# Moving five of eleven modulation rounds of a four-layer kernel: two to a later projection, three to a feed-forward

## The chip, the cores and the metric

One core of a Trainium2 chip runs the whole program. The metric is the device time of one launch in microseconds, median of the runs shown.

## What is computed

Four residual layers act on 256 tokens of width 1024; layers 0 and 1 also carry 256 context tokens, layer 2 uses the context for keys and values only. All is fp32. Each layer has a conditioning vector `c` and a modulation of six rows of 1024, three pairs of which are called rounds 0, 1 and 2 here:

```python
mods = silu(c) @ ada_w[i] + ada_b[i]          # [1024] @ [1024, 6144]
sh1, sc1, g1, sh2, sc2, g2 = split(mods, 6)
h = norm(x) * (1 + sc1) + sh1
x = x + g1 * mixer(h)                         # rounds 0 and half of 1
x = x + g2 * ffn(norm(x) * (1 + sc2) + sh2)   # rest of 1, and 2
```

Mixers and feed-forwards, in order: layer 0, two linear recurrences with one input projection (3616 wide) and a mixture of 32 experts; layer 1, differential attention (projection 3072 wide) and 32 experts; layer 2, latent attention with a Fourier mix, and a dense SwiGLU of width 2816; layer 3, convolutions, and a dense SwiGLU. Rounds (0,1), (0,2), (1,0) and (2,0) are needed for two conditioning vectors (`c` and the context's), all others for one.

## The kernel before, in words

The stages run one after the other; a stage ends for all engines together. Weights come through a ring of six slots of 1 MiB (`self.ring`). The order of everything in the ring is a list that is written at build time (`self.W`, by `plan_...`); SyncE works through it in `feed` (L285 to L295), and before each load it waits until the slot's earlier content is used up. `frees` and `self.released` give slots back in the order in which TensorE's program comes to them.

A round of modulation is eight units of 1 MiB (128 rows of `ada_w`, 2048 columns). Two stages host rounds beside their own projection, both through `st_linear_hosting` (L426): the first projection (called AB here, 28 groups of eight 128x512 matmuls, four groups to a chunk of two ring slots), and the second (called C, 20 groups, the first two chunks of two groups). `hosted` (L384) spreads the units over the groups by a cost of 3, or 5 for a unit of two vectors that VectorE sums. Behind a group, TensorE's program comes to the units given to it:

- a round in `on_pe` is multiplied on TensorE (L471, four matmuls a unit, 32 columns of the array each), and its slot comes free by that;
- any other round is summed on VectorE: `weigh` (L569) takes one instruction of 128x2048 per unit and vector (L575 for the first, L577 for the seven others); the slot comes free when it is done. When all eight are summed, `add_up` (L479) on TensorE adds over the partitions with four matmuls a vector (L486).

Then `take` (L581) adds the bias on VectorE, and GpSimd's queue stores the two rows to a scratch in HBM (L548), after which it may load the next bias (L544). `load_mod` (L608) reads rows back, spread over all partitions, when a later stage needs them: in AB and C by SyncE behind the feed (L525, L526), in the latent attention (L2367) for layer 3. In C, VectorE also normalizes four tiles at the start (L566, L567), and turns angles for rotary embedding at groups 4, 5, 12 and 13 (L808 to L814), in program order with the units.

The AB stage hosts seven rounds (rounds number 0 and 5 of the list on TensorE), C four (number 0 on TensorE). The mixture of experts begins with its own stage (`moe`, L1282): SyncE's loads (L1356, L1360), GpSimd's parameters, and VectorE, whose first act is `mod_here`, a wait for every `load_mod` issued so far.

The feed-forward `ffn` (L2652) has 11 blocks j. TensorE does `gateup(j+1)` (64 records, L2677) and then `down(j)` (16 records, L2689); ScalarE's silu (L2740) and VectorE's product (L2754) lie between. VectorE begins the stage with `entry_begin` (L2564), which needs rows 0 and 1 of layer 3.

A matmul of fp32 stands as two records in the trace, so a group of eight is 16 records.

## Time and profile before

| | |
|---|---|
| median of 3 runs | 2607.36 us (2604.98 to 2614.38) |
| span of the profiled execution | 2609.1 us; no time of its own is recorded for it |
| TensorE busy | 2251.0 us, 86% |
| VectorE busy | 814.0 us, 31% |
| DMA, mean | 268 GB/s |
| AB stage | 59.7 to 292.7 us |
| C stage | 1032.5 to 1195.6 us |
| start stage of the second mixture | 1283.0 to about 1331 us |
| first feed-forward, blocks | 2027 to 2248 us |

The page gives busy times and the span in slices; a stage has its own limits, so the rows below are taken stage by stage. Idle time is that of the named engine ahead of an instruction, with what ended it. `PEclk` is the granted TensorE clock as a share of 2.4 GHz.

### The profile page before, as it was taken

How to read it: one execution, taken by the hardware profiler on the slowest of the kernel's cores; microseconds unless marked ns; L12 is line 12 of the kernel's file. 1: busy time of each engine (PE TensorE's matmuls, PEld its weight loads, DVE VectorE, ACT ScalarE, POOL GpSimd, SP SyncE). 2: the span in 40 equal slices, each digit the busy share in tenths (PEclk: the TensorE clock that was granted, in tenths of full speed). 3: DMA queues.
4: the chain of work that ended last, by engine and by line, in shares of the span. 5: the costliest groups of instructions: out<-in, count | busy, mean ns of one | idle time of the engine just before them, and what ended most of it. 6: DMA issues, size and time to landing. Idle time of an engine off the chain costs nothing. (4 is left out here: it accounts for less than half of the span.)

```text
span 2609.1 us, 35238 instructions
## 1 busy us (share of the span) xinstructions
PE 2251.0 (86%) x14123; PEld 1215.0 (47%) x14124; DVE 814.0 (31%) x1504; ACT 371.3 (14%) x623; POOL 125.7 (5%) x182
## 2 busy tenths in 40 slices
PE   6999969798888882897778788887699999989999
PEld 3333564443343331344442223322455777766776
DVE  2483575520000006375652200000443000393001
ACT  0000222111111111003321111111042000010000
POOL 0000011000000002100100000000210000000000
PEclk8999989899999995999989999999799999999999
DMA  8889712699999984884179999998441544534442
GB/s 286 315 327 349 284 33 67 267 419 423 423 423 422 423 362 171 295 333 187 52 295 423 423 422 423 423 422 370 158 154 41 186 145 161 166 118 130 161 145 81
DMA packets 176765, 698.24 MB, mean 268 GB/s; under 512 B 14085, under 2 KB 72325, under 8 KB 114096
## 3 DMA queue, kind: packets, MB, share of 16 engines
q1 hardware_dynamic: 162512, 648.98, 64.1%
q0 software_dynamic: 8512, 25.83, 3.0%
q10 hardware_dynamic: 5664, 22.37, 2.4%
q8 instruction: 53, 0.87, 0.1%
q14 instruction: 24, 0.20, 0.0%
HBM read 673.87 MB, written 22.20 MB: 267 GB/s over the span
## 5 line engine op out<-in xcount | busy, mean ns | idle before, releaser
L1571 PE MATMUL bank<-ring,arena 128*32 128x512 f32 (+1 forms) x3072 | 357.0, 613 | 76.9 <-DMA ring<-moe_w_up 50.0
L503 PE MATMUL bank<-ring,actT 128*128 128x512 f32 x768 | 344.4, 607 | 11.8 <-issue 7.6
L2677 PE MATMUL bank<-actT,ring 128*128 128x256 f32 x1344 | 293.3, 379 | 0.0
L2677 PEld LDWEIGHTS bank<-actT,ring 128*128 128x128 f32 x1344 | 255.2, 190 | 42.3 <-issue 8.6
L1571 PEld LDWEIGHTS bank<-ring,arena 128*32 128x32 f32 x3072 | 100.5, 112 | 328.4 <-issue 327.1
L1588 PE MATMUL bank<-arena 128*32 128x512 f32 (+1 forms) x2048 | 226.6, 594 | 25.7 <-ACT arena L1662 24.7
L503 PEld LDWEIGHTS bank<-ring,actT 128*128 128x128 f32 x768 | 147.1, 194 | 209.4 <-issue 205.2
L1703 DVE TENSOR_TENSOR arena<-arena,bank 128x512 f32<-128x512 f32 x32 | 22.0, 687 | 612.3 <-ACT arena L1660 612.3
L577 DVE SCALAR_TENSOR_TENSOR arena<-ring,cols,arena 128x2048 f32<-128x2048 f32 x70 | 163.3, 2350 | 58.0 <-DMA ring<-ada_w 56.4
L2039 PEld LDWEIGHTS bank<-arena 128*128 128x128 bf16 x2448 | 141.4, 100 | 32.3 <-issue 26.8
L2689 PE MATMUL bank<-ring,arena 128*128 128x512 f32 x352 | 154.3, 592 | 0.0
L2039 PE MATMUL bank<-arena 128*128 128x128 bf16 x2448 | 147.3, 223 | 4.8 <-DVE arena L1695 4.8
L1588 PEld LDWEIGHTS bank<-arena 128*32 128x32 f32 x2048 | 65.7, 110 | 165.1 <-issue 165.1
L1571 PE MATMUL bank<-actT,arena 128*32 128x512 f32 (+1 forms) x1024 | 116.3, 594 | 30.1 <-DMA actT<-moe_w_up 30.1
L2754 DVE TENSOR_TENSOR arena<-arena,bank 128x512 f32<-128x512 f32 x22 | 15.1, 687 | 402.0 <-ACT arena L2740 402.0
L2689 PEld LDWEIGHTS bank<-ring,arena 128*128 128x128 f32 x352 | 66.9, 190 | 75.7 <-issue 74.6
L1317 PE MATMUL bank<-ring,actT 128*128 128x512 f32 x192 | 83.6, 594 | 4.0 <-DMA arena<-moe_b_rexp 1.8
L1660 ACT ACTIVATE arena<-bank 128x512 f32<-128x512 f32 x32 | 19.1, 597 | 468.4 <-PE bank L1571 468.4
L1571 PEld LDWEIGHTS bank<-actT,arena 128*32 128x32 f32 x1024 | 32.0, 110 | 112.7 <-issue 112.7
L556 ACT ACTIVATE arena<-bank 128x512 f32<-128x512 f32 x48 | 28.7, 597 | 369.1 <-PE bank L503 369.1
L2740 ACT ACTIVATE arena<-bank 128x512 f32<-128x512 f32 x22 | 13.1, 597 | 408.6 <-PE bank L2677 408.6
L1709 DVE TENSOR_TENSOR arena<-bank,mod 128x512 f32<-128x512 f32 x32 | 20.6, 686 | 158.6 <-PE bank L1588 158.6
(446 smaller groups left out, 2045.0 us busy)
## 6 DMA issues: line engine op xcount, KB each, us to landing
ring<-moe_w_gate SPq DMA_DIRECT2D x128, 1024.0 KB, 24.1
arena<-moe_w_down SPq DMA_DIRECT2D x128, 1024.0 KB, 21.8
ring<-ada_w SPq DMA_DIRECT2D x96, 1024.0 KB, 8.0
ring<-ffn_w SPq DMA_DIRECT2D x66, 1024.0 KB, 5.3
ring<-moe_w_up SPq DMA_DIRECT2D x64, 1024.0 KB, 23.8
actT<-moe_w_up SPq DMA_DIRECT2D x64, 1024.0 KB, 24.6
made_scratch<-arena ACTq DMA_DIRECT2D x32, 512.0 KB, 7.7
ring<-ab_w_in SPq DMA_DIRECT2D x14, 1024.0 KB, 7.2
```

The source lines that it names most:

```text
L503: mm = nc.tensor.matmul(self.bank[g % 6][:, :], lhsT(m, k), halves[k // 4][:, k % 4, :], start=(k == 0), stop=(k == KT - 1))
L556: nc.scalar.activation(dest(*groups[g]), self.bank[g % 6][:, :], ACT.Copy).then_inc(self.act_done.up(), 1)
L577: ins = nc.vector.scalar_tensor_tensor(total(n, v), w, c, total(n, v), ALU.mult, ALU.add)
L1317: mm = nc.tensor.matmul(proj_bank(t, c)[:, :], tok(t, 4 * j + k), halves[c][j][:, k, :], start=(j == 0 and k == 0), stop=(j == 1 and k == 3))
L1571: mm = nc.tensor.matmul(bank[j // 2][Q * q:Q * q + Q, :], A(XS + P * kt + Q * q, Q), weights(j, own, q, k * DE, DE), start=(kt == 0), stop ...
L1588: mm = nc.tensor.matmul(bank[4 + half][Q * q:Q * q + Q, :], A(HT + P * (2 * j + f) + Q * q, Q), weights(4 + j, own, q, f * D + half * 512, ...
L1660: nc.scalar.activation(A(SG, 512), bank[0][:, :], ACT.Silu).then_inc(sc["silu"], 1)
L1703: V_.tensor_tensor(A(HH, 512).rearrange("p (j f q) -> p j f q", f=2, q=P), self.by_rows(A(SG, 512)), self.by_rows(bank[1][:, :]), ALU.mult ...
L1709: ins = V_.tensor_tensor(A(YS + half * 512, 512), bank[4 + half][:, :], self.mod_row(5)[:, half * 512:half * 512 + 512], ALU.mult)
L2039: mm = self.nc.tensor.matmul(self.bank[2 + k // 4][:, P * (k % 4):P * (k % 4) + P], part(i)[:, t * D + k * P:t * D + (k + 1) * P], pick[:, ...
L2677: mm = nc.tensor.matmul(bank[2 - 2 * (j % 2) + which][:, f * SEQ:(f + 1) * SEQ], w[:, k, f * P:(f + 1) * P], self.actT[:, k * T:k * T + SE ...
L2689: return nc.tensor.matmul(acc(t, half)[:, :], A(H + 512 * (j % 2) + f * SEQ + t * P, P), w[:, f, half * 512:(half + 1) * 512], start=(j == ...
```

## The change

AB hosts five rounds instead of seven, one of them on TensorE. C hosts the three rounds of layer 2, all on VectorE, the first of them for two vectors. The three rounds of layer 3 are summed on VectorE inside the first feed-forward, from four buffers of their own that GpSimd's queue fills. Layer 3's rows 0 and 1 are now loaded by ScalarE's queue in that feed-forward, and `entry_begin` comes behind its blocks; layer 2's rows 0 and 1 are loaded at the start of the second mixture instead of at the end of C.

```diff
-AB_ROUNDS = [(0, 1), (0, 2), (1, 0), (1, 1), (1, 2), (2, 0), (2, 1)]
+AB_ROUNDS = [(0, 1), (0, 2), (1, 0), (1, 1), (1, 2)]
-C_ROUNDS = [(2, 2), (3, 0), (3, 1), (3, 2)]
+C_ROUNDS = [(2, 0), (2, 1), (2, 2)]
+FFN_ROUNDS = [(3, 0), (3, 1), (3, 2)]
-AB_ON_PE, C_ON_PE = (0, 5), (0,)
+AB_ON_PE, C_ON_PE = (0,), ()
+AB_HOMES, C_HOMES = ((0, 1), (2, 3), (0, 1), (2,), (0,)), ((0, 1), (2,), (0,))
...
     # st_linear_hosting
-        total = lambda n, v: self.A(sums + 2048 * ((on_dve.index(n) % 2) * max(vecs) + v), 2048)
+        total = lambda n, v: self.A(sums + 2048 * homes[n][v], 2048)
...
                     self.load_mod(sp, 1, 2, 6, (0,))
-                    self.load_mod(sp, 2, 0, 2, (0,))
...
     # moe, SyncE
                 if layer == 0:
                     self.load_mod(sp, 1, 0, 2, (0, 1))
+                else:
+                    self.load_mod(sp, 2, 0, 2, (0,))
...
     # mixer_mla, SyncE
-                self.load_mod(sp, 3, 0, 2, (0,))
...
     # ffn, TensorE; CLOSED = (3, 6, 9)
+                def add_up(r, to):
+                    pe.wait_ge(ada_summed.sem, ada_summed.at(KT * (r + 1)))
+                    for b in range(4):
+                        mm = nc.tensor.matmul(to[32 * b:32 * b + 32, :], self.ones[:, 0:32], total[:, 512 * b:512 * b + 512], start=True, stop=True)
+                    mm.then_inc(ada_done.up(), 1)
...
                     if j + 1 < n:
                         gateup(j + 1)
+                    if rounds and j in CLOSED:
+                        pe.wait_ge(h_ready.sem, h_ready.at(j + 1))
+                        add_up(CLOSED.index(j), bank[2 - 2 * (j % 2)])
                     down(j)
+                    if rounds and j in CLOSED:
+                        pe.wait_ge(ada_added.sem, ada_added.at(CLOSED.index(j) + 1))
...
     # ffn, GpSimd
+                def ask(i):
+                    r, k = units[i]
+                    layer, third = rounds[r]
+                    if i >= 4:
+                        pool.wait_ge(ada_summed.sem, ada_summed.at(i - 3))
+                    w = self.I["ada_w_2"][layer % 2]
+                    pool.dma_start(unit(i), w[k * P:(k + 1) * P, 2048 * third:2048 * (third + 1)]).then_inc(self.unit_in[i % 4], 16)
...
+                for r in range(len(rounds)):
+                    for k in range(KT):
+                        ask(KT * r + k)
+                        if k == 4:
+                            bias(r)        # waits for the store of round r-1
+                        if r and k == 2:
+                            store(r - 1)   # waits for take(r-1)
...
     # ffn, ScalarE
+                    if rounds and j == 6:
+                        act.wait_ge(ada_stored.sem, ada_stored.at(32))
+                        self.load_mod(act, rounds[0][0], 0, 2, (0,))
...
     # ffn, VectorE
-                if then_row is not None:
-                    self.entry_begin(dve, link, 0)
                 for j in range(n):
...
+                    if rounds:
+                        if j in CLOSED:
+                            take(CLOSED.index(j), bank[2 - 2 * (j % 2)][:, :])
+                        for i in range(len(units)):
+                            if (0, 0, 1, 1, 1, 2, 2, 2)[i % KT] + 3 * (i // KT) == j:
+                                weigh(i)
+                if then_row is not None:
+                    self.entry_begin(dve, link, 0)
```

## Rows read from the trace of the kernel before

**Rows 1.** Busy time by stretch: PE, PEld, DVE, ACT, POOL, clock, DMA share, GB/s.
```profile
59.70:292.70 233.00, 222.02 (x632) 90.14 (x632) 127.36 (x66) 16.12 (x27) 26.58 (x50) 0.98 0.89 325
125.40:155.50 30.10, 29.34 (x80) 12.59 (x81) 29.48 (x15) 2.38 (x4) 1.16 (x2) 1.00 0.89 317
190.60:222.50 31.90, 31.79 (x72) 13.23 (x72) 23.05 (x11) 1.81 (x4) 3.17 (x6) 0.91 1.00 392
1032.50:1195.60 163.10, 155.39 (x408) 63.52 (x408) 84.26 (x58) 12.84 (x21) 17.75 (x33) 0.96 0.80 291
2048.00:2247.70 199.70, 199.70 (x753) 142.62 (x751) 11.46 (x19) 5.97 (x10) 0.00 (x0) 1.00 0.47 153
```
**Rows 2.** Groups of instructions by line, AB stage.
```profile
L503 PE MATMUL bank<-ring,actT 128*128 128x512 f32 x448 | 201.0, 607 | 10.6 <-issue 7.6 <-DMA ring<-ab_w_in 1.8 <-PEq L628 1.3
L577 DVE SCALAR_TENSOR_TENSOR arena<-ring,cols,arena 128x2048 f32<-128x2048 f32 x49 | 113.9, 2349 | 31.8 <-DMA ring<-ada_w 30.6
L471 PE MATMUL bank<-ring,scx 128*32 128x512 f32 x128 | 15.6, 599 | 1.5 <-DMA ring<-ada_w 1.5
L575 DVE TENSOR_SCALAR arena<-ring,cols 128x2048 f32<-128x2048 f32 x7 | 8.8, 1285 | 48.5 <-DMA ring<-ada_w 48.5
L486 PE MATMUL bank<-arena,misc 128*32 128x512 f32 x24 | 3.2, 600 | 0.0
```
**Rows 3.** Timeline of TensorE in AB: start, length, what, idle before.
```profile
141.91 34.60 PE L503 MATMUL bank<-ring,actT 128*128 128x512 f32 x80
190.65 16.86 PE L503 MATMUL bank<-ring,actT 128*128 128x512 f32 x32 [5.22 <-issue]
263.80 20.84 PE L503 MATMUL bank<-ring,actT 128*128 128x512 f32 x48 [1.80 <-DMA ring<-ab_w_in]
```
**Rows 4.** What SyncE's queue waited for, 60 to 320 us.
```profile
SPq L294 <- DVE arena L577: 97.0, 27, 7.4
```
**Rows 5.** DMA issues of the same stretch; the second row of 60 to 105 us.
```profile
ring<-ada_w SPq DMA_DIRECT2D x52, 1024.0 KB, 7.6
...
mod<-k_ret POOLq DMA_DIRECT2D x1, 2048.0 KB, 13.5
```
**Rows 6.** Groups of instructions by line, C stage.
```profile
L471 PE MATMUL bank<-ring,scx 128*32 128x512 f32 x64 | 9.8, 716 | 7.7 <-DMA ring<-ada_w 7.7
```
**Rows 7.** Timeline of TensorE in C, around its long wait.
```profile
1065.57 1.93 PE L471 MATMUL bank<-ring,scx 128*32 128x512 f32 x8 [7.17 <-DMA ring<-ada_w]
...
1069.90 9.01 PE L503 MATMUL bank<-ring,actT 128*128 128x512 f32 x16
...
1080.69 7.13 PE L503 MATMUL bank<-ring,actT 128*128 128x512 f32 x16
```
**Rows 8.** Timeline of VectorE, C stage.
```profile
1079.65 1.23 DVE L808 TENSOR_TENSOR arena<-arena 128x1024 f32<-128x1024 f32 x1 [37.17 <-ACT arena L556]
```
**Rows 9.** Timeline of VectorE, start of the first mixture, then of the second.
```profile
406.20 2.50 DVE L1421 TENSOR_SCALAR xres<-xres 128x1024 f32<-128x1024 f32 x4 [12.38 <-DMA mod<-mods_scratch]
412.64 1.22 DVE L1424 SCALAR_TENSOR_TENSOR arena<-mod,arena 128x1024 f32<-128x1024 f32 x1 [3.94 <-DMA arena<-moe_b_rexp]
...
1283.00 1.29 DVE L1421 TENSOR_SCALAR xres<-xres 128x1024 f32<-128x1024 f32 x2 [0.37 <-PEq L628]
1295.56 1.23 DVE L1424 SCALAR_TENSOR_TENSOR arena<-mod,arena 128x1024 f32<-128x1024 f32 x1 [11.26 <-DMA arena<-moe_b_rexp]
...
1310.74 0.69 DVE L1439 TENSOR_TENSOR arena<-bank,mod 128x512 f32<-128x512 f32 x1 [0.25 <-PE bank L1317]
```
**Rows 10.** Timeline of SyncE's queue, start of the first mixture.
```profile
396.75 1.15 SPq L612 DMA_DIRECT2D mod<-mods_scratch  x2
```
**Rows 11.** Timeline of TensorE, first feed-forward.
```profile
2075.47 13.98 PE L2677 MATMUL bank<-actT,ring 128*128 128x256 f32 x64
2089.28 7.03 PE L2689 MATMUL bank<-ring,arena 128*128 128x512 f32 x16
```
**Rows 12.** Who waited for whom, 2010 to 2262 us.
```profile
DVE arena L2754 <- ACT arena L2740: 195.6, 11, 20.0
```

More of the change, by code:

```diff
@@ L238, in __init__ @@
         self.cleared = ctx.enter_context(nc.semaphore("cleared"))
+        self.unit_in = [ctx.enter_context(nc.semaphore(f"unit_in{n}")) for n in range(4)]
     def signals(self, *names):
@@ L424, in plan_ada, with st_linear_hosting @@
         self.plan(w[k * P:(k + 1) * P, 2048 * r:2048 * (r + 1)].rearrange("(k p) n -> p k n", p=P), 1, 2048)
-    def st_linear_hosting(self, lhsT, chunks, dest, rounds, sums, on_pe=(), lead=0, unmix=None, tables=None, beside=None):
+    def st_linear_hosting(self, lhsT, chunks, dest, rounds, sums, homes, pick, on_pe=(), lead=0, unmix=None, tables=None, beside=None):
         nc, sm = self.nc, self.sem
@@ L483, in add_up @@
                     for v in range(vecs[n]):
-                        ones = self.ones[:, 0:32] if vecs[n] == 1 else self.A(PICK + 16 * (1 - v), 32)
+                        ones = self.ones[:, 0:32] if vecs[n] == 1 else self.A(pick + 16 * (1 - v), 32)
                         for j in range(4):
@@ L568, in _ @@
                     ins.then_inc(sm["x_normed"].up(), 1)
+                    dve.wait_ge(sm["x_normed"].sem, sm["x_normed"].at(1))
                 def weigh(n, l, r, k):
@@ L586, in _ @@
                 if 2 in vecs:
-                    nc.vector.memset(self.A(PICK, 16), 0.0)
-                    nc.vector.memset(self.A(PICK + 32, 16), 0.0)
-                    nc.vector.memset(self.A(PICK + 16, 16), 1.0)
+                    nc.vector.memset(self.A(pick, 16), 0.0)
+                    nc.vector.memset(self.A(pick + 32, 16), 0.0)
+                    nc.vector.memset(self.A(pick + 16, 16), 1.0)
                 for g in range(len(groups)):
@@ L2252, in raise_sums @@
             nc.scalar.activation(A(LAM, 16), A(LAM, 16), ACT.Exp).then_inc(lam_exp.up(), 1)
-        self.st_linear_hosting(lambda m, k: self.actT[:, k * T + m * P:k * T + m * P + P], C_CHUNKS, dest, C_ROUNDS, C_SUMS, C_ON_PE, lead=2, unmix=A(XX, 2048),
+        self.st_linear_hosting(lambda m, k: self.actT[:, k * T + m * P:k * T + m * P + P], C_CHUNKS, dest, C_ROUNDS, C_SUMS, C_HOMES, C_PICK, C_ON_PE, lead=2, unmix=A(XX, 2048),
                                beside=dict(pool=load_tables, dve=turn_angles, act=raise_sums))
@@ L2650, in plan_ffn, with ffn @@
                 self.plan(I["ffn_w2_2"][l][(j - 1) * H:j * H, :].rearrange("(k p) n -> p k n", p=P), 2, D)
-    def ffn(self, l, then_row):
+    def ffn(self, l, then_row, rounds=()):
         nc, I, A, bank, sm = self.nc, self.I, self.A, self.bank, self.sem
         SG, H = 2048, 3072
+        ada_done, ada_added, ada_bias, ada_stored, ada_summed = (sm[k] for k in ("ada_done", "ada_added", "ada_bias", "ada_stored", "ada_summed"))
+        units = [(r, k) for r in range(len(rounds)) for k in range(KT)]
+        unit = lambda i: A(FFN_UNITS + 2048 * (i % 4), 2048)
+        total = A(FFN_SUM, 2048)
+        kept = self.scx[:, 512:1024]
+        CLOSED = (3, 6, 9)
         acc = lambda t, c: bank[4 + 2 * t + c]
@@ L2747, in _, with weigh, take @@
                 link = self.linker(dve, self.dve_chain)
-                if then_row is not None:
-                    self.entry_begin(dve, link, 0)
+                def weigh(i):
+                    r, k = units[i]
+                    layer = rounds[r][0]
+                    dve.wait_ge(self.unit_in[i % 4], 16 * (i // 4 + 1))
+                    c = self.cols[:, 16 * (layer // 2) + k:16 * (layer // 2) + k + 1]
+                    if k == 0:
+                        ins = nc.vector.tensor_scalar(total, unit(i), c, None, ALU.mult)
+                    else:
+                        ins = nc.vector.scalar_tensor_tensor(total, unit(i), c, total, ALU.mult, ALU.add)
+                    ins.then_inc(ada_summed.up(), 1)
+                    dve.wait_ge(ada_summed.sem, ada_summed.total)
+                def take(r, of):
+                    dve.wait_ge(ada_bias.sem, ada_bias.at(64 * (r + 1)))
+                    dve.wait_ge(ada_done.sem, ada_done.at(r + 1))
+                    nc.vector.tensor_tensor(kept, of, kept, ALU.add).then_inc(ada_added.up(), 1)
                 for j in range(n):
@@ L2755, in _ @@
                                             ALU.mult).then_inc(h_ready.up(), 1)
+                    if rounds:
+                        if j in CLOSED:
[3 more added lines that the diff above has]
+                                weigh(i)
+                if then_row is not None:
+                    self.entry_begin(dve, link, 0)
                 if then_row is not None:
@@ L2995, in run @@
         self.mixer_mla()
-        self.ffn(0, I["norm1_g_2"][1])
+        self.ffn(0, I["norm1_g_2"][1], FFN_ROUNDS)
         self.mixer_conv()
```

22 lines of the change are left out of this document (20 added, 2 removed).

## The prediction

> **What bounds the kernel now.** The page first: TensorE is busy 86% of the span, VectorE 31%, and the DMA mean is far under what the two expert stages reach. That says little, because the change touches only stretches, so I read the busy times by stretch next [rows 1]. In the AB stage TensorE works 222.0 of 233.0 us, in C 155.4 of 163.1 us, in the blocks of the first feed-forward all of 199.7 us. So in all three the end is set by TensorE's own program plus its waits; nothing that only VectorE or the DMA queues do is paid for, unless it makes TensorE wait.
>
> Then the same two hosting stages by line. In AB a group of eight matmuls costs 34.60 / 5 = 6.9 us at full clock [rows 3], 28 of them 194 us; a unit on TensorE is 15.6 / 16 = 0.98 us, an `add_up` of one vector 3.2 / 3 = 1.07 us; VectorE takes 2.35 us per unit and vector, 1.29 us for the first of a round [rows 2]. The rest is waits and slow clock. In the timeline the long wait, 5.22 us, lies ahead of a chunk's first group, and the two groups behind it take 16.86 instead of 13.9 us [rows 3]; the granted clock of that stretch is 0.91 (of 2.4 GHz), after TensorE had stood still [rows 1]. Why the chunk was late: loads are in order, and SyncE stood 97 us for slots that VectorE held [rows 4]; between 125 and 155 us VectorE was busy 29.5 of 30.1 us, and between 190 and 222 us the DMA moved 392 GB/s at a share of 1.00 [rows 1]. First VectorE, then the DMA engines limit the stream; TensorE feels it at the chunks.
>
> **AB stage.** Two rounds go, 16 MiB of 70.
> - Round (2,0) leaves TensorE: 8 x 0.98 = 7.8 us.
> - Round (2,1) leaves VectorE, and its `add_up` TensorE: 1.1 us.
> - Waits, 233.0 - 222.0 = 11.0 us, and 2.9 us of slow clock behind the long one. By the costs in `hosted`, all units together now weigh 152 instead of 200 over the same 26 groups. In the two-vector part that is 1.17 units a group instead of 1.54, 5.5 us of VectorE per 6.9 us instead of 7.2: VectorE keeps up. In the one-vector part it is 8 units and 2 slots of weights per chunk of four groups, 10.5 MB in 27.5 us = 380 GB/s, just under the 392 measured; so I don't expect all waits to vanish. I keep 4 us of the 11 and take 7 + 2.9 = 9.9 us off. Bounds: 0 (nothing of the wait goes) and 13.9.
> Sum AB: 7.8 + 1.1 + 9.9 = 18.8 us. Behind AB everything starts earlier by this; the stage barrier and the stores of the last round follow as before.
>
> **C stage.** Round (2,2) leaves TensorE: the row gives 9.8 us busy and 7.7 us of waits for its eight units [rows 6]; the 7.17 us wait is one of these, and the group behind it took 9.01 instead of 7.13 us [rows 7], 1.9 us. With no unit on TensorE all three go: 19.4 us. Added: four vectors to add up instead of three, 1.07 us. VectorE now sums 32 instead of 24 vector-units, 18.8 us more, but it had stood still 37.2 us at the start of this stage [rows 8] and was busy 84 of 163 us [rows 1].
> What is late next is a chain: a slot of round (2,0) is filled (7.6 us to landing [rows 5]), summed for two vectors (4.7 us), and only then filled again, 12.3 us a turn. Counting the release order, units 1, 3, 5 and 7 form such a chain from the end of the first chunk (1048 us): four turns, 49 us, plus two turns of angles of 3.7 us, 1105 us; TensorE asks for the sum (`add_up` behind group 9) at about 1103 us. A second such chain ends about 2 us ahead of the last `add_up`. Bounds for the stall: 0, and 10 us if each turn meets a queue like the 13.5 us of the big table [rows 5]; I take 3, from the median landing. Sum C: 19.4 - 1.1 - 3 = 15.3 us.
> The Trainium skill, "SBUF — State Buffer", section "The DMA setup-cost knee", has 2 us plus the bytes over 436 GB/s for such a transfer, 4.4 us for a unit; by that estimate a turn is 9.1 us, the stall is zero, and the total would be 3 us better. The trace's 7.6 us is a median with other loads in flight, and I go by it.
>
> **Feed-forward.** TensorE's blocks have no gap: 13.98 and 7.03 us follow each other [rows 11]. Three `add_up`s go in between: 3 x 1.07 = 3.2 us, all on the path. The rest lies beside: VectorE waited 195.6 us of the stage [rows 12]; per block of 20.7 us it now gets at most three units, 7.1 us. In blocks 3, 6 and 9 it also stands in `take` until `gateup(j+1)` and `add_up` are through, but the next product is needed only after `down(j)` and another `gateup`, over 20 us later, and `take` itself (0.7 us) ends inside `down(j)` (7 us), before TensorE waits for it. DMA: 3 MiB per block more, 153 + 152 GB/s of the 392 seen; a ring load has two blocks of lead. `entry_begin` moves behind the blocks, where VectorE waits for `down(10)`; its rows are loaded from block 6 on, four blocks early. The removed load in the latent attention was in nobody's way: 0. Bounds: 3.2 and, if each `add_up` also costs a handshake as long as `take` and its silu-to-product step, 6.
> Here a page speaks against the change. First the row: the first product of a unit takes 1285 ns, the other kind 2349 ns for the same 2048 columns [rows 2]. The Trainium skill, "SBUF — State Buffer", section "SBUF: two separate sides", says that DMAs issued by GpSimd can't get their descriptors written while VectorE runs in its faster two-port modes. By that rule three instructions of 1.29 us could hold back unit loads, 3.9 us if all of it reached TensorE, total 2584 us; by the slack above it is zero, and I take zero.
>
> **Second mixture.** The load of rows 0 and 1 of layer 2 used to lie at the end of C; now it is issued when the stage starts, ahead of the two expert loads, and VectorE's first act waits for it. The first mixture shows just this: two half loads, together as large, issued at 396.75 us [rows 10]; VectorE went on at 406.20 us, and the parameters behind were in at 412.64 us, 15.9 us after the start [rows 9]. In the second they were in 12.6 us after the start (1283.0 to 1295.56 us) [rows 9]. So parameters come 3.3 us later, and VectorE's chain of normalizing, transposing and routing has 0.25 us of slack against TensorE's projection [rows 9]. Cost 3 us; bounds 0 and 4.
> The added wait for VectorE's own instruction in C (`x_normed`) is one semaphore, 0.1 us at most: nothing.
>
> **Sum.** 18.8 + 15.3 - 3.2 - 3 = 27.9 us, 1.07%. The profiled span is 2609.1 us, 1.7 over the median of the runs shown; I take the gain off both: span 2581 us, median 2607.4 - 27.9 = 2579.5 us.
>
> **Rivals.**
> - *The summing chain bounds C.* For: (2,0) with two vectors comes first there, ropes lie between its units, and the chain above had no slack. Against: VectorE has idle time. Priced with 10 us of stall at the first and 4 at the second sum, C gives 4.3 us, total gain 16.9: 2590 us.
> - *AB's waits stay.* For: 380 GB/s needed is near 392 reached, and late chunks bring slow clock with them. Against: a fifth fewer units in every stretch. AB gives 8.9 us only, gain 18.0: 2589 us.
> - *All cover holds.* No wait left in AB, no stall in C, the mixture's parameters not delayed: 22.8 + 18.3 - 3.2 = 37.9 us, 2569.5 us.
> - *The units come too slowly in the feed-forward (slower than before).* GpSimd's queue feeds 24 MiB there; a unit is due every 6.9 us (20.7 / 3). The one large load of that queue took 13.5 us for 2 MiB [rows 5], 6.8 us per MiB if one followed the other, hardly under the limit. If they serialize and take 10 us each, a block is 30 instead of 20.7 us, eight blocks lose 74 us: 2654 us. It decides from about 6.9 us per unit in series; slower than before it is from 8.4 us on. Against: four units may be in flight, so one may take 25 us from ask to sum, and the DMA share in the stage is 0.47 [rows 1]. The descriptor rule above would be a cause for it, but 3.9 us in all don't reach it.
>
> **How the numbers follow.** Forecast 0.68, chain in C 0.13, waits in AB 0.09, all cover 0.06, slow units 0.04. The measurement tells about 0.5% (13 us) from no change. Forecast and full cover are faster (0.74); the two that halve the gain are faster by 17 to 18 us in their middle, and I count 0.13 of their 0.22 as over 13 us: faster 0.87, same 0.09, slower 0.04. The range 2566 to 2596 holds all the forecast's bounds that don't fall together and the two halved cases.
>
> **What would show it.** AB about 214 us long, without the low clock near its fourth chunk; no TensorE instruction at the on-array unit line in C, and C about 148 us; the wait ahead of `add_up` in C under 5 us; in the feed-forward three short matmul groups and no idle TensorE, blocks else at 20.7 us; in the second mixture a wait of 9 to 12 us for the modulation load and routing some 3 us later after its stage's start. It is wrong if TensorE waits for sums or products in the feed-forward, if C is over 155 us, or if AB keeps its 11 us of waits.

## The result, and the profile after

The changed kernel takes 2572.2 us (median of 4 runs, 2568.0 to 2578.8), the kernel before beside it 2607.5 us (4 runs, 2605.0 to 2614.4). The ratio is 0.9865, 95% interval 0.985 to 0.988: 35.3 us less, clear of noise though under 2%. The forecast was 2579.5 us, 27.9 us faster, in a range of 2566 to 2596.

| | before | after |
|---|---|---|
| span of the profiled execution | 2609.1 us | 2566.2 us (its time 2568.0 us) |
| TensorE busy | 2251.0 us | 2226.7 us |
| VectorE busy | 814.0 us | 865.3 us |
| DMA, mean | 268 GB/s | 272 GB/s |

Busy time by stretch after: AB, C, the blocks of the first feed-forward. The columns are those of [rows 1].
```profile
58.70:269.30 210.60, 210.58 (x560) 88.11 (x560) 108.47 (x55) 16.14 (x27) 20.21 (x38) 0.99 0.76 277
1008.50:1156.40 147.90, 143.95 (x352) 61.41 (x352) 100.37 (x68) 12.85 (x21) 15.77 (x27) 0.99 0.73 262
2001.70:2205.30 203.60, 203.60 (x777) 142.92 (x776) 63.45 (x45) 5.97 (x10) 18.00 (x33) 1.00 0.74 262
```
In AB the 11.0 us in which TensorE stood still are gone to the last tenth, and its clock is 0.99. In C it stands still 4 us in all. In the feed-forward it still never does, though the DMA share went from 0.47 to 0.74.

TensorE in AB around what was the long wait, after; it answers to [rows 3].
```profile
154.74 48.33 PE L508 MATMUL bank<-ring,actT 128*128 128x512 f32 x112
203.00 1.92 PE L491 MATMUL bank<-arena 128*32 128x512 f32 x16
204.86 27.73 PE L508 MATMUL bank<-ring,actT 128*128 128x512 f32 x64
```
Seven groups in 48.33 us are 6.9 us each, and no row carries a bracket with idle time.

TensorE in C, after; it answers to [rows 7].
```profile
1008.48 27.70 PE L508 MATMUL bank<-ring,actT 128*128 128x512 f32 x64 [1.15 <-PEq L1905]
1037.31 41.44 PE L508 MATMUL bank<-ring,actT 128*128 128x512 f32 x96 [1.12 <-DMA ring<-c_w_qkv]
...
1081.56 3.22 PE L491 MATMUL bank<-arena 128*32 128x512 f32 x16 [2.82 <-DVE arena L583]
1084.70 34.96 PE L508 MATMUL bank<-ring,actT 128*128 128x512 f32 x80
```
The wait of 7.17 us for `ada_w` has gone with its instruction. New are 1.12 us for a weight, and 2.82 us for VectorE ahead of the first `add_up`.

VectorE in C, after, at the start of the sums.
```profile
1040.08 9.27 DVE L583 SCALAR_TENSOR_TENSOR arena<-ring,cols,arena 128x2048 f32<-128x2048 f32 x4 [19.07 <-DMA ring<-ada_w]
1049.71 4.62 DVE L583 SCALAR_TENSOR_TENSOR arena<-ring,cols,arena 128x2048 f32<-128x2048 f32 x2 [0.36 <-DMA ring<-ada_w]
```
It had the first unit of (2,0) early and stood 19 us for the second, then found the next ones ready: what was late was one landing.

DMA issues between 1005 and 1045 us, after: how many, KB each, median us to landing.
```profile
ring<-ada_w SPq DMA_DIRECT2D x3, 1024.0 KB, 17.1
arena<-xres POOLq DMA_DIRECT2D x4, 256.0 KB, 3.9
ring<-c_w_qkv SPq DMA_DIRECT2D x1, 1024.0 KB, 14.7
arena<-c_lq POOLq DMA_DIRECT2D x2, 256.0 KB, 8.2
arena<-c_lk POOLq DMA_DIRECT2D x2, 256.0 KB, 11.3
scx<-ada_b POOLq DMA_DIRECT2D x4, 64.0 KB, 10.2
```
A unit took 17.1 us here against the 7.6 us of [rows 5]; GpSimd's own transfers (tables, the residual, biases) were in flight beside it.

TensorE in the first feed-forward, after; it answers to [rows 11].
```profile
2049.96 13.98 PE L2690 MATMUL bank<-actT,ring 128*128 128x256 f32 x64
2063.86 1.07 PE L2723 MATMUL bank<-arena,misc 128*32 128x512 f32 x8
2064.86 7.13 PE L2702 MATMUL bank<-ring,arena 128*128 128x512 f32 x16
```
The first `add_up` lies between `gateup` and `down`; the two others look the same.

VectorE, then TensorE, at the start of the second mixture, after; they answer to [rows 9].
```profile
1249.02 1.30 DVE L1429 TENSOR_SCALAR xres<-xres 128x1024 f32<-128x1024 f32 x2 [6.13 <-DMA mod<-mods_scratch]
1257.79 1.23 DVE L1432 SCALAR_TENSOR_TENSOR arena<-mod,arena 128x1024 f32<-128x1024 f32 x1 [7.47 <-DMA arena<-moe_b_rexp]
```
```profile
1243.27 13.97 PE L1323 MATMUL bank<-ring,actT 128*128 128x512 f32 x32 [1.10 <-PEq L634]
1257.73 14.00 PE L1323 MATMUL bank<-ring,actT 128*128 128x512 f32 x32 [0.49 <-DMA arena<-moe_b_rexp]
```
The parameters are in 14.5 us after the stage's start (1243.27 us), 12.6 us before the change.

Lengths of the stretches, from TensorE's timelines: each runs from its first matmul to the first of the next stretch, so it holds the barrier behind it too and is a little longer than the windows above. M1 is the second mixture's start up to the first matmul that gathers tokens for the experts, MLA the latent attention up to the feed-forward's blocks.

| kernel | AB | C | M1 | MLA | FFN blocks | span |
|---|---|---|---|---|---|---|
| before | 234.4 | 165.7 | 48.5 | 193.3 | 223.2 | 2609.1 |
| after | 212.4 | 149.7 | 50.1 | 186.7 | 226.9 | 2566.2 |
| forecast of the difference | -18.8 | -15.3 | +3 | 0 | +3.2 | -27.9 |
| measured | -22.0 | -16.0 | +1.6 | -6.6 | +3.7 | -42.9 |

The remaining 3.6 us lie in stretches without an edit (each differs by up to 2.8 us, both ways). One of them is more than scatter: in the first mixture TensorE waits 3.3 to 3.9 us for the parameters in all seven kernels whose AB hosts five rounds with one of them on TensorE, and 1.7 to 2.1 us in the other seven (3.79 in after, 1.81 in before); in after the two groups behind it also take 15.70 instead of 14.00 us. The change costs 2 to 3 us there, which the forecast does not have; what delays the load is open. The MLA stretch was between 186.7 and 193.5 us long in the profiles of the fourteen kernels of this study, which in it differ by one load that nobody waits for, so I don't count its 6.6 us to the change. The edited stretches give 32.7 us; the medians differ by 35.3. Edited stretches vary as well: AB is 209.4 to 212.4 us long in the seven kernels that have after's AB, and C 148.0 to 149.7 in the three that have after's C (after, one_buffer, two_buffers). Much of that is the clock at a stage's start: AB's first group took 8.89 us in before and 10.16 in after, where 7.11 is the shortest, and C's first took 8.91 in before, where after's first four took 6.9 each.

### The profile page after: what moved, and what is told of

Read it like the earlier page. It is cut to its first block and busy times, and to the rows that moved or that the text cites. A ratio compares the mean times of both kernels' runs of the same rounds, so it can differ in the third digit from the quotient of the medians.

```text
span 2566.2 us, 35098 instructions
## 1 busy us (share of the span) xinstructions
PE 2226.7 (87%) x14019; PEld 1206.6 (47%) x14020; DVE 865.3 (34%) x1531; ACT 371.1 (14%) x623; POOL 140.3 (5%) x206
## 5 line engine op out<-in xcount | busy, mean ns | idle before, releaser
L508 PE MATMUL bank<-ring,actT 128*128 128x512 f32 x768 | 336.9, 599 | 4.0 <-PEq L634 1.8
L2831 DVE TENSOR_TENSOR arena<-arena,bank 128x512 f32<-128x512 f32 x22 | 15.1, 687 | 297.0 <-ACT arena L2799 297.0
L1323 PE MATMUL bank<-ring,actT 128*128 128x512 f32 x192 | 85.6, 605 | 6.5 <-DMA arena<-moe_b_rexp 4.3
L2799 ACT ACTIVATE arena<-bank 128x512 f32<-128x512 f32 x22 | 13.1, 597 | 410.9 <-PE bank L2690 410.9
```

The source lines that it names most:

```text
L508: mm = nc.tensor.matmul(self.bank[g % 6][:, :], lhsT(m, k), halves[k // 4][:, k % 4, :], start=(k == 0), stop=(k == KT - 1))
L1323: mm = nc.tensor.matmul(proj_bank(t, c)[:, :], tok(t, 4 * j + k), halves[c][j][:, k, :], start=(j == 0 and k == 0), stop=(j == 1 and k == 3))
```

## The experiments

"Before" and "after" stand for the two kernels. Kernels that were timed together share their runs of before: 2606.1 us (11 runs) for the first four; 2609.3 (17) for unit_earlier, one_buffer, two_buffers and mod_early; 2607.2 (9) for both, quiet_start, combined and combined_all. The lengths of all of them:

| kernel | AB | C | M1 | FFN blocks | span | ratio to before |
|---|---|---|---|---|---|---|
| c_hosts_six | 209.4 | 213.2 | 50.1 | 223.3 | 2630.5 | 1.012 (1.0103 to 1.0137) |
| ab_keeps_seven | 234.6 | 142.6 | 49.9 | 226.9 | 2585.2 | 0.9929 (0.9915 to 0.9942) |
| small_loads | 225.8 | 163.8 | 50.5 | 223.2 | 2623.4 | one run |
| one_vector | 234.6 | 166.2 | 50.2 | 223.2 | 2603.4 | one run |
| unit_earlier | 232.1 | 165.3 | 48.5 | 223.2 | 2607.2 | 0.9987 (0.9978 to 0.9997) |
| both | 221.6 | 166.5 | 48.5 | 223.2 | 2590.6 | one run |
| one_buffer | 210.9 | 148.7 | 50.2 | 236.1 | 2582.7 | one run |
| two_buffers | 211.0 | 148.0 | 50.2 | 226.9 | 2570.5 | one run |
| mod_early | 211.0 | 147.8 | 50.5 | 226.9 | 2572.7 | 0.9878 (0.986 to 0.9896) |
| quiet_start | 211.6 | 146.3 | 50.1 | 226.9 | 2571.1 | one run |
| combined | 209.4 | 146.1 | 50.4 | 226.9 | 2569.1 | 0.9861 (0.9843 to 0.9879) |
| combined_all | 206.3 | 146.6 | 50.6 | 226.9 | 2564.6 | 0.985 (0.9831 to 0.9869) |

### Is the feed-forward the better host? (c_hosts_six)

```diff
-C_ROUNDS = [(2, 0), (2, 1), (2, 2)]
+C_ROUNDS = [(2, 0), (2, 1), (2, 2), (3, 0), (3, 1), (3, 2)]
-self.ffn(0, I["norm1_g_2"][1], FFN_ROUNDS)
+self.ffn(0, I["norm1_g_2"][1])
```


> The changed kernel with layer 3's three rounds in the second projection (C, now six rounds, all on VectorE) and none in the feed-forward. My theory: C is then bound by its stream. 48 units and 12 weight slots are 63 MB, 157 us at the 400 GB/s seen, and VectorE has 56 x 2.35 = 132 us of sums plus some 28 us of its own; so the stage goes from 149.7 us to 165 to 175, the feed-forward gets its 3.7 us back, and the total is 12 to 21 us over the changed kernel, about 2584 to 2593. Rival: the feed-forward is only a parking place and VectorE's idle time in C would have covered the sums; then C stays within 3 us and the total is some 3 us under the changed kernel, 2569.

Measured: 2635.5 us; C is 213.2 us, 63.5 more than with three rounds. The expectation missed it by over 40 us, the stage by 38. TensorE's waits in C, from its timeline:
```profile
1065.60 3.64 PE L491 MATMUL bank<-arena 128*32 128x512 f32 x16 [10.40 <-DVE arena L583]
1091.98 8.70 PE L508 MATMUL bank<-ring,actT 128*128 128x512 f32 x16 [7.78 <-DVE scx L590]
...
1144.34 9.82 PE L508 MATMUL bank<-ring,actT 128*128 128x512 f32 x16 [8.44 <-DVE scx L590]
...
1176.18 9.27 PE L508 MATMUL bank<-ring,actT 128*128 128x512 f32 x16 [7.09 <-DVE scx L590]
```
L590 is `take`. A round now closes every three or four groups, and TensorE, which may not go on with the projection until an earlier round's bank has been taken, stands behind a VectorE that is still summing the next units; each of the three stops shown is followed by a group of 8.7 to 9.8 us instead of 7.1. VectorE has hardly any slack left itself: of the 213 us it is busy 155.5 and stands 39.0 for units to land. So the feed-forward is the better host by 59.8 us, and that is measured; why is in part argued. Over 60 us between two sums, own buffers beside the ring, and a VectorE with time to spare all come with that place, and no run takes them apart.

### The parts added one by one (ab_keeps_seven)

```diff
-AB_ROUNDS = [(0, 1), (0, 2), (1, 0), (1, 1), (1, 2)]
+AB_ROUNDS = [(0, 1), (0, 2), (1, 0), (1, 1), (1, 2), (2, 0), (2, 1)]
-C_ROUNDS = [(2, 0), (2, 1), (2, 2)]
+C_ROUNDS = [(2, 2)]
```


> The changed kernel with all seven rounds left in the first projection as before (two of them on TensorE), one round in C and three in the feed-forward: the change without the relief of AB. My theory: AB is the larger half of the gain, so AB is 234 us again instead of 212.4, C with one light round about 143 instead of 149.7, total 15 us over the changed kernel, about 2587, which is 20 us under the kernel before. Rival: the gain comes from taking work out of C and from quieter DMA later on, AB alone is worth little; then the total is within 5 us of the changed kernel.

Measured: 2587.6 us, AB 234.6, C 142.6. The two rounds that leave AB take 234.6 - 212.4 = 22.2 us with them and cost C 149.7 - 142.6 = 7.1 us; the difference, 15.1 us, agrees with that of the medians, 2587.6 - 2572.2 = 15.4 (16.7 by the ratios, each to its own runs of before). AB's long wait stands where it stood, with 5.35 us.

### What made AB wait? (small_loads, one_vector, unit_earlier, both)

My prediction said: first VectorE, which holds the slots, then the DMA engines. Three kernels take one supposed cause each out of the kernel before.

small_loads leaves out three quarters of each unit that AB hosts (so later sums have other values, tokens go to other experts, and only the AB column can be compared):
```diff
+            if i in self.ab_units:
+                dst, src = dst[:, :, 0:512], src[:, :, 0:512]
```


> The kernel before, in which the hosted units of the first projection load only 512 of their 2048 columns, all instructions kept; three quarters of seven rounds' modulations are therefore not the reference's, and so the experts' routing may differ: only the length of the AB stage (234.4 us before, first group to the next stage's first matmul) is read. If the bytes of the stream make TensorE wait, its 11 us of waits and the slow clock behind them go: 220 to 222 us. If the slots that VectorE holds for its sums make it wait, most stay: 228 us or more.

one_vector leaves the second vector's products and sums out in AB:
```diff
-                    for v in range(vecs[n]):
+                    for v in range(1 if unmix is None else vecs[n]):
```


> The kernel before, in which VectorE sums only the first vector of the two-vector rounds of the first projection (the context's modulation is left wrong, so routing may differ; only the AB stage is read); loads as before, 40 instead of 56 vector-units. If VectorE's holding of slots is what delays the weights, the waits go: 220 to 224 us. If the bytes do, the stream still asks 390 GB/s in the second half and the 5 us wait ahead of a chunk stays: 230 us or more.

unit_earlier computes all, with one unit behind group 14 instead of group 15:
```diff
+        if groups == 28 and len(rounds) == 7:
+            share[14], share[15] = share[14] + 1, share[15] - 1
```


> The kernel before, in which one hosted unit of the first projection moves from behind group 15 to behind group 14 (3 and 2 instead of 2 and 3); nothing else. Theory of slot order: slots are given back in program order, and with three units behind the last group of a chunk the second half of the next chunk's weights gets a slot of the chunk in work, which is free only when that is done; so the 5.2 us wait ahead of group 16 and the slow clock behind it (2.9 us) come from that alone, and the AB stage falls from 234.4 to 226 to 228 us, the total by 6 to 8 us to about 2599. Rival: the wait is the bytes or VectorE; then moving one unit by one group changes under 1 us.

TensorE ahead of the chunk after the long one, in before; then the long waits in small_loads, in one_vector and, with the one that follows, in unit_earlier.
```profile
223.97 7.10 PE L503 MATMUL bank<-ring,actT 128*128 128x512 f32 x16 [1.53 <-issue]
```
```profile
186.72 15.67 PE L506 MATMUL bank<-ring,actT 128*128 128x512 f32 x32 [5.23 <-issue]
```
```profile
189.88 16.05 PE L503 MATMUL bank<-ring,actT 128*128 128x512 f32 x32 [6.00 <-issue]
```
```profile
186.17 13.97 PE L505 MATMUL bank<-ring,actT 128*128 128x512 f32 x32 [0.90 <-issue]
...
220.90 9.31 PE L505 MATMUL bank<-ring,actT 128*128 128x512 f32 x16 [5.83 <-issue]
```
Half of VectorE's work on the two-vector rounds gone: the wait is 6.00 instead of 5.22 us, AB as long as before. So VectorE's hold on the slots was not the cause, and that step of the prediction is wrong. Less data: the small waits for loads are gone (one of 0.83 us for ScalarE is left), and the long one stays, 5.23 against 5.22 us; AB is 225.8 us, between the two expectations. One unit moved by one group: the long wait is 0.90 us, and the two groups behind it run at full clock (13.97 instead of 16.86 us); but now the next chunk is late, 5.83 instead of 1.53 us, and only 2.3 us of stage are left as gain where 6 to 8 were expected, 0.13% of the kernel, which the interval just tells from nothing.

Why one group matters is in the list of loads. By the costs in `hosted`, three units stand behind group 15, the last of its chunk. With the two slots of the chunk in work and the first half of the next that is all six slots, so the next chunk's second half could be asked for only when the chunk in work was through; TensorE then waits for that load, whatever VectorE or the bytes do. The trace of before shows it: SyncE's second load of weights (184 to 185.7 us), and what its queue waited for between 170 and 195 us.
```profile
185.47 0.38 SPq L294 DMA_DIRECT2D ring<-ab_w_in  x1
```
```profile
SPq L294 <- PE bank L503: 8.3, 1, 8.3
```
The last group of the chunk ended at 178.30 + 7.13 = 185.43 us, the load was issued at once and landed in 5.1 us: that is the wait of 5.22. VectorE was not behind then; at 179.61 and 182.18 us it stood itself for units. The table of [rows 4], which gave the prediction its 97 us, also has waits on these matmuls (45.9 us in 7 times), and the prediction passed over them. Behind this wait lies the second limit, the bytes. If both are all there is, taking both away leaves nothing:

> The kernel before with the two earlier edits together: the seventeenth hosted group gets one unit more and the next one less, and the hosted one-vector and two-vector units bring only 512 of their 2048 columns (the instructions stay, so sums are not those of the reference). If the waits of the first stage have two causes that cover for each other (slot order at the chunk of group 16, bytes at the chunk of group 20 and at the later ones), no wait over 0.7 us and no slow stretch stay behind the stage's start, and it is 234.4 - 11 - 3 = 220 us long (217 to 223). If one cause stands behind all, it is as with the better of the two alone, 226 us. If a third one (VectorE's pace) takes over, waits stay at group 16 or 24 and it is above 226 us.

Measured: AB 221.6 us. The only wait of TensorE inside AB in both:
```profile
250.23 20.84 PE L508 MATMUL bank<-ring,actT 128*128 128x512 f32 x48 [0.86 <-ACT arena L561]
```
The two edits by themselves save 2.3 and 8.6 us, together 12.8: the two causes cover for each other, and there is no third of any size. The stage's first group hides part of it: it took 8.89 us in before, 7.11 in small_loads, one_vector and unit_earlier, 10.17 in both. Without that group the savings are 0.5 and 6.8 us, together 14.1. The change removes both at once, since `hosted` then puts at most two units behind any group, and 16 MiB fewer come. That is why no wait at all was left.

### How much cover do the units have in the feed-forward? (one_buffer, two_buffers)

```diff
-unit = lambda i: A(FFN_UNITS + 2048 * (i % 4), 2048)
+unit = lambda i: A(FFN_UNITS + 2048 * (i % 1), 2048)     # i % 2 in two_buffers
-                    if i >= 4:
-                        pool.wait_ge(ada_summed.sem, ada_summed.at(i - 3))
+                    if i >= 1:
+                        pool.wait_ge(ada_summed.sem, ada_summed.at(i))
```


> The changed kernel with one buffer instead of four for the units in the first feed-forward. A unit then costs its landing and its sum in series, 9.9 + 2.35 = 12.3 us or, without others in flight, some 6 + 2.35 = 8.4 us, where one is due every 6.9 us. Theory: 24 units take 200 to 290 us instead of the 186 us of nine blocks, so the feed-forward (226.9 us) grows by 30 to 100 us, and TensorE waits for sums and products. Rival: VectorE's slack of 20 us per block is enough to hide even that; then it stays within 3 us.

> The changed kernel with two buffers instead of four. A unit may then take (9.9 + 2.35) / 2 = 6.1 us, just under the 6.9 us at which it is due. Theory: the feed-forward stays within 3 us of 226.9 us, so four buffers are more cover than is needed. Rival: the waits of GpSimd's queue for the stores between rounds break the flow, and it grows by 5 to 20 us.

Units of `ada_w` from GpSimd's queue between 1990 and 2260 us, with one, two and four buffers.
```profile
arena<-ada_w POOLq DMA_DIRECT2D x23, 1024.0 KB, 5.4
```
```profile
arena<-ada_w POOLq DMA_DIRECT2D x22, 1024.0 KB, 6.7
```
```profile
arena<-ada_w POOLq DMA_DIRECT2D x20, 1024.0 KB, 9.2
```
Two buffers: 226.9 us, as with four. One: 236.1 us, 9.2 more, where I had expected at least 30. With one buffer each unit costs 5.4 us of landing and 2.35 us of sum, 24 x 7.75 = 186 us, still under the 200 us of the blocks. VectorE stands 126.8 us for units and comes late to a product (L2831) that TensorE waits for ahead of two `add_up`s:
```profile
2138.26 1.94 PE L2723 MATMUL bank<-arena,misc 128*32 128x512 f32 x8 [4.30 <-DVE arena L2831]
...
2206.28 1.07 PE L2723 MATMUL bank<-arena,misc 128*32 128x512 f32 x8 [1.83 <-DVE arena L2831]
```
The waits are 6.1 us; a slower `add_up` and `down` behind the first (1.94 and 9.15 us) make up the rest. The expectation took 9.9 us, the landing with four in flight, for its high end and some 6 us for its low end, and its 30 us of growth are more than even its own 200 - 186 us give. Two buffers are not as good as four for VectorE, whose wait for units grows from 3.3 to 34.0 us; only TensorE does not feel it. VectorE's waits with two buffers and with four, between 1975 and 2225 us:
```profile
DVE arena L2818 <- DMA arena<-ada_w: 34.0, 14, 4.8
```
```profile
DVE arena L2818 <- DMA arena<-ada_w: 3.3, 4, 1.1
```
For the rival of slow units: it was to decide from 6.9 us per unit in series. With one buffer a unit costs 7.75 us in series, beyond that bound, and TensorE pays 9.2 us, not 24 x 0.85 = 20. The bound was too strict: the code asks for eight units in three blocks, 62 us, which is 7.75 us a unit.

### The load at the second mixture (mod_early)

```diff
                     self.load_mod(sp, 1, 2, 6, (0,))
+                    sp.wait_ge(ada_stored.sem, ada_stored.at(32))
+                    self.load_mod(sp, 2, 0, 2, (0,))
```
(and no load at the mixture's start)

> The changed kernel with the load of layer 2's rows 0 and 1 back at the end of the second projection (behind a wait for their store). Theory: at the start of the second mixture the load holds up the parameters and VectorE, so that start stage (50.1 us from its first matmul to the first expert's) falls to 48 us and the 0.5 us wait of TensorE there goes; total 1.5 to 3 us less. Rival: 48.5 and 50.1 are only two draws of one length; then it stays within 49 to 51 us.

Measured: 2575.3 us, M1 50.5 us, no gain. TensorE at the start of the mixture, in mod_early and in before:
```profile
1241.81 29.69 PE L1325 MATMUL bank<-ring,actT 128*128 128x512 f32 x64 [1.10 <-PEq L636]
```
```profile
1283.00 27.70 PE L1317 MATMUL bank<-ring,actT 128*128 128x512 f32 x64 [1.10 <-PEq L628]
```
The wait for parameters is gone (0.74 and 2.36 us ahead of the transposes, as before, where after has 1.21 and 2.74), and 1.6 us with it. But the projection itself takes 2.0 us longer, behind the same idle 1.10 us and with the same instructions. The granted clock is 0.86 in its first 14.2 us, where before and after have 1.00. The two later kernels with this edit show the same (29.66 and 29.86 us). But the edit need not be the cause: small_loads and one_vector, which have before's mixture, took 29.68 and 29.41 us with the clock at 0.86 and 0.88, and unit_earlier and both took 27.70. So the start stage without the load is 48.5 us long at full clock and 50.2 to 50.6 at the slow one; the delay that I priced at 3 us costs 1.6 against the first and nothing against the second, and taking it away brought nothing here.

### C's late landing, and a better version (quiet_start, combined, combined_all)

```diff
                     pool.wait_ge(sm["x_normed"].sem, sm["x_normed"].at(1))
+                    pool.wait_ge(self.pe_done.sem, self.pe_done.at(3))
```


> The changed kernel, with GpSimd's own transfers at the start of the second hosting stage held until TensorE has done its third group. If these transfers are what made the second unit of (2,0) land 17 us after its issue, it now lands within 9 us, VectorE's wait of 19 us for it falls to 10 or less, TensorE's waits of 1.12 us (c_w_qkv) and 2.82 us (sum of (2,0)) go, and the stage is 145 to 147 us instead of 149.7. If the ring's own loads crowd each other, the landing stays at 15 us or more and the stage at 148 to 150 us. Held too long, the table's late arrival would show as VectorE waiting for it at the angles of group 4.

Measured: C 146.3 us, 3.4 less than after, but 1.7 less than two_buffers, which has after's C. VectorE waits 9.14 us for the second unit, not 19.07, and later 8.57 us for another:
```profile
1032.01 9.27 DVE L584 SCALAR_TENSOR_TENSOR arena<-ring,cols,arena 128x2048 f32<-128x2048 f32 x4 [9.14 <-DMA ring<-ada_w]
1049.84 4.61 DVE L584 SCALAR_TENSOR_TENSOR arena<-ring,cols,arena 128x2048 f32<-128x2048 f32 x2 [8.57 <-DMA ring<-ada_w]
```
```profile
1010.37 68.91 PE L508 MATMUL bank<-ring,actT 128*128 128x512 f32 x160 [1.18 <-PEq L1906]
1081.69 1.92 PE L491 MATMUL bank<-arena 128*32 128x512 f32 x16 [2.42 <-DVE arena L584]
```
The second unit's landing was crowded by GpSimd's transfers: VectorE waits 18.0 to 19.7 us for it in the four kernels that have three rounds in C and keep them at the start (after, mod_early, one_buffer, two_buffers), 9.1 to 11.2 in the three that hold them. The crowding then falls on a later unit. The unit behind the 8.57 us, SyncE's queue and its landing, between 1030 and 1038 us, while GpSimd issued its held transfers from 1031.8 us on:
```profile
1036.65 0.33 SPq L299 DMA_DIRECT2D ring<-ada_w  x1
```
```profile
ring<-ada_w SPq DMA_DIRECT2D x1, 1024.0 KB, 13.1
```
The weight's wait and the slower `add_up` (3.22, now 1.92 us) are gone, but not by this edit: one_buffer and two_buffers have neither, with GpSimd's transfers where after has them. The wait for the sum stays, 2.42 us here, 2.54 and 2.18 in those two. TensorE in two_buffers:
```profile
1083.73 1.92 PE L491 MATMUL bank<-arena 128*32 128x512 f32 x16 [2.18 <-DVE arena L583]
```
So half of the expectation missed, and how much of the 3.4 us is the edit's is not shown; the kernel was also timed only once. What is left of the stall is VectorE's own program: from 1049.7 to 1081.5 us it has no idle time in after, nor in quiet_start from 1049.8 to 1081.7 (five units of two vectors 23.1, angles 7.5, a copy 1.2 us). Only one turn of a slot lies ahead of that, unit 3 in the slot of unit 1.

combined also asks for that sum one group later and has the load of mod_early:
```diff
+        lag = lambda n: 2 if unmix is not None and n == 0 else 1
-            return [n for n in on_dve if g == min(last_group[n] + 1, len(groups) - 1)]
+            return [n for n in on_dve if g == min(last_group[n] + lag(n), len(groups) - 1)]
```


> The changed kernel with three small edits: the load of layer 2's first rows back at the end of the second hosting stage, the first add_up of that stage one group later, and GpSimd's transfers there held for three groups. Theory: the first is worth 1.6 us in the second mixture (less whatever slow clock comes with it), the other two together the 3.9 us of waits in the second hosting stage. Sum 4 to 6 us: 2567 us beside the kernel before at 2607, ratio 0.9845 (0.983 to 0.9865). Rival: the waits move to the next chunk, as in the experiment that gave a unit one group earlier; then the ratio is that of the change alone, 0.9865.

Measured: 2571.8 us, 2570.0 to 2573.5. In C TensorE has no wait left:
```profile
1010.39 77.21 PE L510 MATMUL bank<-ring,actT 128*128 128x512 f32 x176 [1.18 <-PEq L1908]
```
and C is 146.1 us, 3.6 less than after, 1.9 less than two_buffers; the mixture gives nothing, as above. 0.9861 against 0.9865 for the change alone: 1 to 4 us of gain can't be told from run to run differences.

combined_all takes the last round off TensorE in AB:
```diff
-AB_ON_PE, C_ON_PE = (0,), ()
+AB_ON_PE, C_ON_PE = (), ()
```


> The kernel of the run ahead, and in the first stage round (0,1) too is summed on VectorE, so none of its units is on TensorE. On TensorE go 8 units of 0.98 us, and two add_up vectors of 1.07 us come: 5.7 us less if VectorE keeps up. VectorE gets 8 units of two vectors, 37.6 - 2.1 = 35.5 us more in a stage of 212 us. Theory: five rounds leave it room, the stage is 206 us long (205 to 208), ratio 0.982 to 0.984. Rival: the two-vector rounds at the start then come faster than VectorE sums them (4.7 us each against 1.17 units in 6.9 us is 5.5, but the slots wait in order), chunks come late as before the change, and the stage is 215 us or longer: ratio 0.9865 or above.

Measured: 2569.3 us, 2563.3 to 2572.0. AB is 206.3 us, VectorE busy 143.1 us of it, and one wait has come:
```profile
58.10:264.40 206.30, 201.09 (x512) 86.27 (x512) 143.08 (x71) 16.72 (x28) 21.92 (x38) 1.00 0.77 283
```
```profile
205.06 27.70 PE L510 MATMUL bank<-ring,actT 128*128 128x512 f32 x64 [3.40 <-issue]
```
The ratio, 0.985, lies just above the 0.982 to 0.984 expected. The wait lies ahead of group 20 (8 + 6 + 6 groups of 16 records come before it), and in this kernel `hosted` puts three units behind group 19, the last of its chunk: the slot order of the experiments above again. The second half of the next chunk's weights was issued at 199.85 us, 0.03 us after that group ended, and landed in 5.1 us. The stage is as short as expected all the same, 3.1 us shorter than in combined. Its median is the lowest of the study, 38 us under before, but the interval of its ratio overlaps that of the change: it may be better by some 3 us, and that is not shown.

## Why the prediction was right, step by step

**TensorE's own program sets the three stages.** Right: the busy time in AB fell by 222.0 - 210.6 = 11.4 us, where the removed units, the `add_up` and the slow clock were put at 7.8 + 1.1 + 2.9 = 11.8. The difference is within what the stage's first group varies (8.9 us before, 10.2 after, 7.1 in combined).

**AB's waits: right in direction, wrong in cause and in size.** The sentence "First VectorE, then the DMA engines limit the stream" fell: halving VectorE's two-vector work changed nothing (one_vector). The long wait came from the order of the slots and the small ones from the bytes (unit_earlier, small_loads, both). "I keep 4 us of the 11" was the mis-sized term. It measured nothing: no wait is left. It rested on 380 GB/s needed in the one-vector part against 392 reached; that part shows 331 GB/s at a share of 0.82 (205 to 233 us) and no wait. Bytes under the limit cost nothing here once the slots came free in time. AB as a whole is 3.2 of the 4.8 us by which the edited stretches beat the forecast; its slower first group (10.16 against 8.89 us) hides 1.3 us more.

**C.** The removed part was right: no instruction at the on-array unit line, no 7.17 us wait behind it. "I take 3" for the stall of the sum measured 2.8 us, and two small items came beside it, 1.1 us for a weight and 1.3 us of slow `add_up` (3.22 against 1.92 us). The chain of four slot turns was not what set it. The sum was asked for at 1081.56 - 2.82, 70 us after the start, as forecast (1103 - 1032.5 = 70.5), and was ready at 73, as forecast too (1105 - 1032.5 = 72.5), but by another way: a landing of 17 us instead of 7.6, one slot turn, and then 31.8 us of VectorE's program without a gap. That is the mechanism of the first rival, with a stall of 3 us and not of 10. And the late landing is not what the stall hangs on alone, since it stays at 2.4 us with the unit 10 us earlier. That the stall met the forecast at 3 us is luck. So is some of the 16.0 us: 1.8 of them are the slow first group that before had in C.
By the setup-cost rule of the Trainium skill ("SBUF — State Buffer", "The DMA setup-cost knee") a unit would land in an estimated 4.4 us and the stall be zero. The trace has 5.4 us for a unit with no other of its queue in flight, 9.2 with up to four, and 17.1 in C's start; the rule counts one transfer and none beside it, and the stall was there.

**Feed-forward.** 3.2 us were forecast and 3.7 measured: three `add_up`s of 1.07 us, and `down` behind each takes 7.13 instead of 7.03 us. VectorE stood in `take` for TensorE 61.2 us in all, the wait of up to 20.4 us that the prediction had put beside the path, and TensorE never waited for it. The table of waits of the stage, 1975 to 2225 us, shows it:
```profile
DVE arena L2831 <- ACT arena L2799: 90.6, 8, 13.4
DVE scx L2825 <- PE bank L2723: 61.2, 3, 20.4
```
Of the 195.6 us of [rows 12], 90.6 are left: the cover was used, not used up, and two_buffers shows that TensorE is as well served with half of the buffers. The prediction's 6.9 us per unit was too short, though: by the schedule in the code a unit is due every 7.75 us, and with that the rival would be slower than before from some 8.9 us, not 8.4 (27.9 us of gain over 24 units are 1.16 us each; with 6.9 the same sum gives 8.1, so the 8.4 was off as well). The descriptor rule of the Trainium skill ("SBUF — State Buffer", "SBUF: two separate sides") had an estimated 3.9 us at risk here; VectorE waited 3.3 us for units in the whole stage, and no gap reached TensorE, so no run here shows it costing time.

**Second mixture.** 1.6 us instead of 3, and even that only against before's 48.5 us; kernels without this load also took 50.2 and 50.5 (see mod_early). The parameters came 1.9 us later (14.5 against 12.6 us after the start), not 3.3 as the first mixture's 15.9 us suggested, and 0.3 us of that stayed in the slack. Why the first mixture's two half loads took longer than this single one, no run isolates. The 2 to 3 us that the first mixture's start grew by are not in the forecast at all.

**The rest.** 6.6 us of the span's difference lie in the latent attention and belong to neither kernel; it is a difference between two executions. The forecast of the gain in the median was 7.4 us short: 4.8 us are its own errors in the edited stretches, and 2.6 us lie outside them.

**The rivals.** Full cover (2569.5 us) was nearest in AB; it fails in C, where the stall is there. Waits that stay (AB) and slow units (feed-forward) are excluded by after's own rows. The first rival was near in kind and wrong in size: VectorE's sums do set the first `add_up` in C, at a stall of 2 to 3 us, and the second one waits for nothing.

## What to carry to other kernels

A wait ahead of a load in an ordered ring has two readings, too many bytes or a slot that can't be free yet; count the slots at the late load (in work, units behind the last group, halves of the next) before blaming an engine or the bandwidth, and expect the one to cover for the other. Work for an idle engine can cost little in one stage and much in another: three rounds cost 3.7 us in the stage that closes one every 60 us, has buffers of its own for them and leaves VectorE idle, and 63 us in the one that closes one every three or four groups through the shared ring. Which of these counts most is not shown. A gain of a few us in one stretch has to be read from that stretch, since an untouched one of 190 us varied by 7, and beside more than one kernel that shares it: quiet_start gained 3.4 us against one and 1.7 against another.

## What the runs showed of the hardware

- The same 64 records behind the same 1.10 us of idle time took 27.70 us in before, unit_earlier and both and 29.41 to 29.86 us in five other kernels, with a granted clock of 0.85 to 0.88 in the first 14.2 us of these five, against 1.00. The six kernels with a wait of 0.25 to 0.6 us in the middle all had full speed (13.97 and 14.00 us). What makes it isn't settled.
- A 1 MiB transfer of 128 rows landed in 5.4, 6.7 and 9.2 us with one, two and four buffers in its queue, beside the same ring loads; the ring's own went from 5.3 us in before to 7.8 with four. More in flight still paid for VectorE: it stood 126.8, 34.0 and 3.3 us for units.
- At C's start small transfers of another queue (64 to 256 KB each, 13 of them) beside a 1 MiB load made it land in 17.1 us; with them held back, VectorE's wait for it was 9.14 instead of 19.07 us, and a unit issued among them later took 13.1 us.
